# One layer of a hybrid encoder: gate factors moved into the experts' rows, the last two experts' rows kept on chip, the tail's loads moved forward

## The reference, cut to what matters

```python
g = argmax(x @ w_router_group)                      # 1 of 4 groups, probability pg
top_v, top_i = top_k(logits_e[rows, g], 2)          # 2 of 8 experts in that group
gate = softmax(top_v) * pg                          # two gate values per token
for e in range(32):
    xb = x[tokens of e]                             # blocks of up to 128 rows
    y_e = (silu(xb @ w_g[e]) * (xb @ w_u[e])) @ w_d[e]
out[token] = gate_0 * y_0 + gate_1 * y_1            # the token's two experts
x = layer_norm(ALPHA * x + out, ln3_g, ln3_b)
```

## Time and profile before

| | before |
|---|---|
| median of 3 runs | 1645.26 us |
| the profiled execution | 1648.83 us |
| span in its trace | 1647.0 us |
| TensorE busy | 1571.5 us, 95% |
| VectorE busy | 1018.3 us, 62% |
| ScalarE busy | 783.7 us, 48% |
| GpSimd busy | 261.3 us, 16% |
| mean granted TensorE clock | 0.98 |

### The profile page before, as it was taken

How to read it: one execution, slowest core, us unless ns; L and a number is a source line. 1 busy time by engine, 2 the same in 40 slices (tenths; PEclk the granted TensorE clock), 3 DMA queues, 4 the chain that set the end, 5 groups by cost and what they waited for, 6 DMA issues and landing times.

```text
span 1647.0 us, 21343 instructions
## 1 busy us (share of the span) xinstructions
PE 1571.5 (95%) x8472; PEld 1314.8 (80%) x8472; DVE 1018.3 (62%) x1336; ACT 783.7 (48%) x1105; POOL 261.3 (16%) x219
## 2 busy tenths in 40 slices
PE   8999999899998999999999988999999999999956
PEld 6877887788876888999877767888888888888842
DVE  5611111677755556222544548999989989999936
ACT  4411021544445012222422223888888888888824
POOL 0000000300035571000122211111111111111005
PEclk9999999999999999999999987999999999999988
DMA  9721111700021545100345445999999999999877
GB/s 350 257 75 39 41 56 59 250 20 20 3 89 60 226 136 216 66 26 14 128 149 177 161 166 189 378 388 394 384 404 387 393 392 394 387 396 392 322 268 290
DMA packets 85989, 351.72 MB, mean 214 GB/s; under 512 B 23410, under 2 KB 28146, under 8 KB 64132
## 3 DMA queue, kind: packets, MB, share of 16 engines
q1 hardware_dynamic: 75764, 330.43, 53.0%
q0 software_dynamic: 9216, 18.89, 3.0%
q10 hardware_dynamic: 912, 1.05, 0.3%
HBM read 321.93 MB, written 43.15 MB: 222 GB/s over the span
## 4 chain that ended last, share of the span: by engine, by line
PE 90%; DVE 3%; ACT 3%; DMA 2%; issue 1%; POOL 0%; SPq 0%; DVEq 0%; POOLq 0%; ACTq 0%
PE M L1302 26%; PE M L1019 11%; PE T L822 6%; PE M L795 6%; PE T L1302 5%; PE M L899 4%; PE T L731 3%; PE T L1363 2%; PE M L731 2%; PE T L1093 2%; PE T L1091 2%; PE T L1092 2%; PE M L1125 2%; PE M L1107 2%; PE T L1421 2%; DVE rounded L1845 1%
## 5 line engine op out<-in xcount | busy, mean ns | idle before, releaser
L1845 DVE TENSOR_TENSOR rounded<-beside,rounded 128x1024 fp32r<-128x1024 f32 (+1 forms) x397 | 472.9, 1236 | 55.1 <-ACT rounded L1731 41.2
L1302 PE MATMUL M<-rounded 128*128 128x512 f32 x1908 | 461.2, 392 | 2.8 <-ACT rounded L1766 1.9
L1302 PEld LDWEIGHTS M<-rounded 128*128 128x128 f32 x1908 | 355.9, 188 | 77.3 <-ACT rounded L1766 2.1
L1731 ACT CAST rounded<-beside 128x1024 fp32r<-128x1024 f32 x256 | 260.0, 1050 | 72.1 <-DMA beside<-in_w_exp_up 59.6
L1019 PE MATMUL M<-rounded 128*128 128x512 f32 x816 | 196.6, 395 | 2.8 <-ACT rounded L1601 1.6
L1019 PEld LDWEIGHTS M<-rounded 128*128 128x128 f32 x816 | 150.1, 188 | 33.7 <-issue 2.0
L1741 ACT CAST rounded<-beside 128x1024 fp32r<-128x1024 f32 x128 | 128.4, 1051 | 24.8 <-DMA beside<-in_w_exp_down 15.7
L1845 DVE TENSOR_TENSOR rounded<-T,rounded 128x512 fp32r<-128x512 f32 (+2 forms) x98 | 92.6, 948 | 36.8 <-ACT rounded L1614 17.6
L1302 PE MATMUL T<-rounded 128*128 128x512 f32 x384 | 108.7, 398 | 0.0
L2504 POOL DMA_INDIRECT expert_rows<-beside,route_out x32 | 38.9, 1217 | 345.1 <-ACT beside L1772 328.5
L731 PEld LDWEIGHTS T<-tables,arena 128*128 128x128 f32 x548 | 64.3, 143 | 27.7 <-issue 8.8
(11 more groups left out here) (365 smaller groups left out, 2436.1 us busy)
## 6 DMA issues: line engine op xcount, KB each, us to landing
beside<-in_w_exp_gate SPq DMA_DIRECT2D x64, 1024.0 KB, 7.6
beside<-in_w_exp_up SPq DMA_DIRECT2D x64, 1024.0 KB, 10.3
beside<-in_w_exp_down SPq DMA_DIRECT2D x32, 2048.0 KB, 11.3
arena<-x_rows SPq DMA_DIRECT2D x27, 512.0 KB, 4.9
x_rows<-arena SPq DMA_DIRECT2D x18, 512.0 KB, 3.8
arena<-expert_rows SPq DMA_DIRECT2D x9, 1024.0 KB, 13.3
arena<-in_x_prompt SPq DMA_DIRECT2D x16, 512.0 KB, 3.9
arena<-in_cache_mem_k SPq DMA_DIRECT2D x8, 1024.0 KB, 5.6
```

The costliest lines, as they stand in the source:

```text
L1302: got = nc.tensor.matmul(out, x[xs], (high, low)[ws](w)[:, c:c + 512], start=(first and n == 0), stop=(last and n == 2))
L1731: nc.scalar.copy(as_both(high(c)), both_raw(c)).then_inc(gu_high, 1)
L1845: return nc.vector.tensor_tensor(out, x, highs.bitcast(f32), ALU.subtract)
```

## The change

- VectorE computes the gate values, with 1/ALPHA in them, before expert 0's splits of chunks 4 to 7, and multiplies them into `r_hot`. TensorE turns that into `slot_gate`, a gate value per slot and expert, with 18 f32 products of 32 columns; the unused products drop from 20 to 12. `results` multiplies by it when it leaves PSUM.
- Experts 30 and 31 are no longer scattered (unless further blocks follow). Their gated rows stay in `xT_parts[0]` and `xT_parts[1]` as rounded high and low parts. GpSimd builds 18 one-hot matrices `hots` during expert 28 (`mark_last_rows`), and TensorE adds the rows to each of the nine tiles (`rows_of_last`, eight rounded products a tile). The rows of `expert_rows` that nobody writes are zeroed by one DMA of 9.4 MB early on.
- x2 tiles are loaded as soon as the last gate and up weights are split; pair tiles as soon as the scatters of experts 28 and 29 have landed and their places are free. `xl`, `yk`, gain and shift lie elsewhere.
- Pairs need no gate in the tail. They are added to x2 by GpSimd for tiles 0, 1, 2 (two adds each), by VectorE for tiles 3, 4, and by TensorE with the identity (four f32 products) for tiles 5 to 8. The order of the tiles is 0 to 8. gain and shift go to PSUM behind the second square.

```diff
@@ SP, early
             sp.wait_ge(pads_ready, 1)
+            sp.dma_start(ye_dram.rearrange("(p a) (h c) -> p (a h) c", p=P, c=CW),
+                         conv_w[:, 2, :].unsqueeze(1).to_broadcast([P, 4 * NT, CW])).then_inc(pairs_zeroed, 16)
             sp.dma_start(u_dram[0:2, :], zero_row).then_inc(edge_out, 16)
@@ SP, tail
-            sp.wait_ge(gu_used, 8 * more + 8 * NE)
-            ... nine x2 tiles, gain3, shift3
-            sp.wait_ge(ye_out[1], 16 * (NE // 2))
-            sp.wait_ge(ye_out[0], 16 * more + 16 * (NE // 2))
-            ... nine pair tiles
+            def load_pairs(t):
+                if t < PT:
+                    sp.wait_ge(gu_used, 8 * more + 8 * (NE - 1) + t + 1)
+                else:
+                    sp.wait_ge(xgT_ps, more + NE)
+                sp.dma_start(yk[t], ye_pairs[t * P:(t + 1) * P, :, :]).then_inc(last_in[t], 16)
+            sp.wait_ge(gu_low, 8 * more + 8 * NE)
+            for t in range(PT):
+                load_x2(t)
+            sp.wait_ge(ye_out[0], 16 * (NE // 2 - 1))
+            load_x2(PT)
+            sp.wait_ge(ye_out[1], 16 * (NE // 2 - 1))
+            for t in range(2):
+                load_pairs(t)
+            sp.dma_start(gain3, A["ln3_g"].to_broadcast([P, D])).then_inc(ln_in, 16)
+            for t in range(2, 6):
+                load_pairs(t)
+            sp.wait_ge(down_low, 4 * more + 4 * NE)
+            sp.dma_start(shift3, A["ln3_b"].to_broadcast([P, D])).then_inc(ln_in, 16)
+            for t in range(6, NT):
+                load_pairs(t)
@@ TensorE, before the experts
-            for _ in range(20):
+            for _ in range(12):
                 nc.tensor.matmul(M[0][:, 0:512], sel_slot[:, 0, 0, :], sel_slot[:, 0, 0:4, :], start=True, stop=True)
+            pe.wait_ge(sel_ready, 3)
+            for k in (0, 1):
+                for t in range(NT):
+                    to_slots = sel_slot[:, k, t, :] if t < PT else sel_last[:, k, 0, :]
+                    got = nc.tensor.matmul(T[1][:, 0:NE], to_slots.bitcast(f32), r_hot[:, k, t, :], start=(k == 0 and t == 0), stop=(k == 1 and t == PT))
+            got.then_inc(rank_ps, 1)
@@ TensorE, tail
-            ... diag products of the seven tiles of BY_PE
+            def rows_of_last(e, t):
+                for part in (0, 1):
                     for c in (0, 512):
+                        got = nc.tensor.matmul(T[t % 2][:, c:c + 512], hots[e][t], xT_parts[e][part][:, c:c + 512],
+                                               start=(e == 0 and part == 0), stop=(e == 1 and part == 1 and t not in BY_PE))
+                return got
+            pe.wait_ge(hots_ready, NT + 1)
+            pe.wait_ge(ye_rows, NE - 1)
+            rows_of_last(0, 0)
+            rows_of_last(0, 1)
+            pe.wait_ge(ye_rows, NE)
+            for t in range(NT):
+                if t > 1:
+                    pe.wait_ge(sum_done, NORMS + t - 1)
+                    rows_of_last(0, t)
+                got = rows_of_last(1, t)
+                if t in BY_PE:
+                    pe.wait_ge(last_in[t], ROWS_IN[t])
+                    for k in (0, 1):
+                        for c in (0, 512):
+                            got = nc.tensor.matmul(T[t % 2][:, c:c + 512], ident, yk[t][:, k, c:c + 512], start=False, stop=(k == 1))
                 got.then_inc(picks_ps, 1)
@@ ScalarE
-                nc.scalar.copy(yo[u], M[1][:, :]).then_inc(ye_rows, 1)
+                nc.scalar.mul(yo[u], M[1][:, :], gate).then_inc(ye_rows, 1)
+            act.wait_ge(down_used, 4 * NE - 4)
+            nc.scalar.mul(xT_parts[0][0], M[1][:, :], slot_gate[:, NE - 2:NE - 1]).then_inc(gates_ready, 1)
+            for c, used in ((0, 4 * NE - 2), (512, 4 * NE)):
+                act.wait_ge(down_used, used)
+                nc.scalar.mul(xT_parts[1][0][:, c:c + 512], M[0][:, c:c + 512], slot_gate[:, NE - 1:NE]).then_inc(gates_ready, 1)
@@ VectorE, tail
+            dve.wait_ge(gates_ready, NT + 1)
+            nc.vector.scalar_tensor_tensor(xT_parts[0][1], M[1][:, :], slot_gate[:, NE - 2:NE - 1], xT_parts[0][0].bitcast(f32),
+                                           ALU.mult, ALU.subtract).then_inc(ye_rows, 1)
+            def last_low(half):
+                cols = slice(half * 512, half * 512 + 512)
+                dve.wait_ge(gates_ready, NT + 2 + half)
+                return nc.vector.scalar_tensor_tensor(xT_parts[1][1][:, cols], M[0][:, cols], slot_gate[:, NE - 1:NE],
+                                                      xT_parts[1][0][:, cols].bitcast(f32), ALU.mult, ALU.subtract)
+            def add_pairs(n):
+                t = BY_DVE[n]
+                dve.wait_ge(last_in[t], ROWS_IN[t])
+                nc.vector.tensor_tensor(xl[t], xl[t], yk[t][:, 0, :], ALU.add).then_inc(pairs_step, 1)
+                dve.wait_ge(pairs_step, 1 + 2 * n + 1)
+                nc.vector.tensor_tensor(xl[t], xl[t], yk[t][:, 1, :], ALU.add).then_inc(pairs_step, 1)
             with dve.If(more > 0):
...
+            with dve.Else():
+                add_pairs(0)
+                last_low(0)
+                add_pairs(1)
+                last_low(1).then_inc(ye_rows, 1)
@@ GpSimd
+            def mark_last_rows():
+                for e in (0, 1):
+                    for t in range(NT):
+                        got = nc.gpsimd.tensor_scalar(hots[e][t], iota, patch_tok[:, e, t:t + 1], None, ALU.is_equal)
+                return got
+                if b == NE - 4:
+                    pool.wait_ge(plan_ready, 1)
+                    mark_last_rows().then_inc(hots_ready, 1)
+            for t in BY_POOL:
+                pool.wait_ge(last_in[t], ROWS_IN[t])
+                nc.gpsimd.tensor_tensor(xl[t], xl[t], yk[t][:, 0, :], ALU.add).then_inc(pool_step, step.next())
+                pool.wait_ge(pool_step, step.value())
+                nc.gpsimd.tensor_tensor(xl[t], xl[t], yk[t][:, 1, :], ALU.add).then_inc(pairs_added, 1)
```

172 lines of the change are left out of this document (95 added, 77 removed).

## The result

The changed kernel takes 1660.31 us (median of 4 runs, 1658.78 to 1664.21), the kernel before, run beside it, 1646.57 (4 runs, 1645.1 to 1648.59): a ratio of 1.0089, 95% interval 1.0074 to 1.0103, so 13.7 us slower, where + 8.8 was forecast. The profiled execution of the changed kernel took 1664.21 us, the longest of its four, with a span of 1662.2 for the 1647.0 before.

The account below looks back on a forecast made before the run. TensorE bounds the kernel until 1590.3 us, then two DMA round trips, then TensorE again. The tail's + 6.3 and the start's + 2.5 sum to + 8.8, giving 1654.1 us on the median; range 1646 to 1662.

Parts of the forecast that it names:

- The sign and the path: Whole run: slower, chance 0.77; TensorE idles after the last down product until VectorE's last low half, then sets the pace.
- T0: Moment TensorE may take expert 31's rows, behind VectorE's last low half: 1608.8 us, two of four additions blocked.
- the landing: Pairs arriving by DMA before VectorE's additions: tile 3 at 1598.5 us, tile 4 at 1601.
- its later end: Tail: VectorE's and GpSimd's pair additions alternate strictly, so TensorE may take expert 31 only at 1609.8 us.
- The forecast's slower case: Pair loads: the first ten us keep 240 GB/s, so tile 4's pairs land at 1602.2 us.
- The tail from T0: After TensorE may take expert 31: 30.5 us of tiles, 5.3 each for 5 to 8, then 14.0 behind the last sum.
- The start of the experts: Before expert 0: 18 new narrow products, eight fillers fewer; shift 1.3 to 4.5 us, taken as + 2.5.
- The marks: Expert 28: 18 GpSimd one-hot builds of 0.3 to 0.8 us, 0.45 taken; VectorE's loss counted as hidden, 0.
- Rival (c): Exposed cover: one-hot builds stall TensorE in expert 28, or zeroing at 200 GB/s delays the first stage; + 14 to + 20; chance 0.10.
- Zeroing and gate factor: Early 9.44 MB store, free above 250 GB/s, some 10 us at 200; gate multiply on ScalarE off the path, 0.

Follow-up runs that it names:

- order and sums: Changed kernel with the last expert's low halves ahead of VectorE's pair additions, and those additions placed where their tiles' sums are wanted: 1654.64 us, ratio 1.0051.
- The best version measured: Kernel with the order, sums and x2 edits, 8 fillers and tile 2 on TensorE, its 18 marks made one expert later: 1645.31 us, ratio 0.9993.

## Why the prediction was right, and where it wasn't

**The sign and the path.** Right: TensorE until the last down product, then idle until VectorE's last low half, then the tail at its own pace. TensorE's idle time of 18.3 us took the place of the two round trips of the earlier trace rows.

**T0 and the landing.** The time from the landing of tile 3's pairs to T0 (TensorE's first product of expert 31's rows, 1617.42) was forecast as 10.3 (two of four additions blocked by 2.05) and was 10.16, with blocks of 0.4, 2.0 and 1.5 on three of them. That the sum of the blocks came out (3.9 for 4.1) is partly luck, since the blocks are not the assumed ones. The trace is strict alternation, which the forecast had as its later end, at 11.3: each of VectorE's three blocked additions ended 1.1 us after the GpSimd addition beside it, and each of GpSimd's two 2.2 us after VectorE's. So it is at every such meeting in the eight traces that have one (33 stretched additions, all within 0.02 us of 1.08 or 2.20). It took 10.16 and not 11.3 because GpSimd's additions stood otherwise against VectorE's than drawn: the blocks drawn were 1.0, 2.4 and 1.7. The Trainium skill's page "SBUF — State Buffer", section "Who interferes with whom", calls this an exclusive lock, and the trace agrees.

The landing itself was mis-sized: 1598.5 forecast, 1607.26 measured, which is 1601.0 after taking off the 6.2 by which the whole stage was late. Its first six us ran at 305 GB/s, and until the landing 13.0 MB had moved (the windows summed), where my count for tile 3 was 12.05: six tiles of pairs are issued within 5 us, and it seems that part of tile 4 moved with tile 3. The forecast's slower case had an error of its own: ten us at 240 GB/s from 1568.9 on and 425 after that give 1604.1 for tile 4, not 1602.2. Measured, less the 6.2, it is 1603.5. At the 358 GB/s that the Trainium skill's page "DMA: Bandwidth & Descriptors", Specifications, gives per core the queue can't have been held: the windows show 415 to 419. So T0 came 2.4 later than forecast, and that is all the error of the tail.

**The tail from T0.** 30.5 forecast, 30.7 measured; 5.3 a tile on TensorE for tiles 5 to 8; 14.0 behind the last sum, 14.07 measured. Tail in all: + 6.3 forecast, + 9.0 measured, the landing being the difference. Against the other trace of the kernel before's tail it would be + 11.5, so 9.0 is not known to better than that.

**The start of the experts.** + 2.5 forecast, + 2.5 measured in the changed kernel, and this too is partly luck. The forecast had 1.3 without a fall of the clock and 4.5 with one, and took a value between. Measured, the turn of the rows starts 1.6 later (narrow products at full clock, 4.10 for 36 records, 4.0 forecast), the first products of expert 0, cold, add 1.5, and 0.6 comes back within expert 0, which the sum didn't have. By the measure in which the changed kernel has 3.1, the eleven other profiles with the narrow products show 2.8 to 5.9, 3.3 in the middle: the value taken is the usual one, and the upper end does occur.

**The marks.** Hidden in the changed kernel, as forecast, but for a wrong reason. The price was 0.45 and is 0.6 at the least and 1.4 in the mean. The step that failed is "more than an expert of 17.3 to spare": I set the gather's lead against marks of 14 us at most. They took 24.5, the lead fell from 33.7 to 14.0, and a gather lands after 9.1 in the median and 11.4 at most, so 2.6 us were left. With the low halves first the lead was 12.0 and the slowest landing 12.0. One execution of a variant went beyond, for 8.5 us. Rival (c) was a narrow miss rather than a remote case.

**Zeroing and gate factor.** Hidden: the store landed 28.2 us after its issue, at 98, with 12 to spare until 110.7, and the kernel with the zeroing alone is at 0.9995.

**The clock.** Not foreseen: the execution's own dips. For the profiled execution the sum was short by 6.4 (15.2 for 8.8): 3.7 ahead of the experts, where the clock fell, and 2.7 in the tail, 2.5 of it the landing. Between the medians it was short by 4.9 (13.7 for 8.8). The tail's 2.7 is part of that; the other 2.2 are within the 2.5 by which the kernel before's tail differs between its two traces, and aren't told apart further.

**Where the gain of the change went.** Two round trips are gone from the chain, but the landing that replaces them is a queue of 13 MB, the wanted rounding is queued behind that landing, GpSimd's additions stretch VectorE's, and TensorE has 4.6 us more to do (30.7 for 26.1). Each of the first three was undone: x2 rows behind the pairs 5.6 to 7.2 of the tail, order and sums 6.5, tile 2 off GpSimd some 4. Together they bring the tail from 66.1 to 49.7 (51.3 with the last down product at full clock), under the 57.1 and 54.5 of the kernel before. What stays is the start: 3 us or more for 36 narrow records and the clock they cost. The best version measured is at 0.9993 (0.9978 to 1.0008), no difference from the kernel before.

## What to carry to other kernels

An instruction of 0.7 us that another engine waits for must not stand behind a DMA wait it doesn't need; and if it is moved, what the next buffers wait for (here the sums) must move with it, or the stop only changes its place and the cold clock is paid again. Where additions of VectorE and GpSimd with both operands in SBUF meet, price them as taking turns. Where a queue is full, count every byte that was issued ahead of the wanted one and price the landing as bytes by rate. When work is put ahead of a gather on a queue, compare its stretched length, beside the engine it shares with, with the gather's lead less its slowest landing, not with the time until its use.

## What the runs showed of the hardware

- The same stretch of the same program runs at 1.00 or at 0.50 of TensorE's clock from one execution to the next, once TensorE has stopped for a moment. At 304 us, behind stops of 1.45 and 0.8 us that every trace has, it is at half in four of fourteen. At the router's end the profiles lie from - 2.6 to + 4.8 us around the one before; a difference of one profile's span under some 5 us says nothing without the shift by stages.
- 36 narrow products of 32 columns, back to back, cost the clock in all twelve profiles that have them. In nine it falls to half 0.3 to 2.3 us before their end, although TensorE doesn't stop; in three it falls 2 us behind them, at a stop of 1.10 that leaves the clock at full in the kernel before.
- VectorE's and GpSimd's additions of two operands in SBUF wait for each other in turn: the one that is met ends 1.1 us (VectorE) or 2.2 us (GpSimd) after the other's end, however early it had begun itself (alone they take 1.2 and 2.35). GpSimd's other operations stretch as well: 0.6 to 2.5 for a mark of 128x128, 0.55 to 1.5 for a root of 128x1.
- The core's DMA engines moved 415 to 419 GB/s for over 20 us with loads of x2 rows, gain and pairs from the chip's memory.
